# Norm statistics as token columns, spread to rows by TensorE, and two panels multiplied together behind each norm

## The chip, the cores and the metric

The kernel runs on one core of a Trainium2 chip. The metric is the device time of one execution in microseconds, the median of several runs. Lower is better.

## The reference, cut to what matters

The reference is one inference step of a two-layer decoder: 512 prompt tokens and 8 sample tokens, 1024 channels. Only the norms and the products behind them matter here:

```python
def rmsnorm(x, g):
    xf = x.astype(F32)
    y = xf * lax.rsqrt(jnp.mean(xf * xf, axis=-1, keepdims=True) + EPS)
    return y.astype(x.dtype) * g
...
for l in range(DEPTH):                      # two layers
    ...
    o = jnp.concatenate([seq_out, mem_out], axis=-1) @ p['w_out'][l]
    x = x + rmsnorm(o, p['norm_mix_post'][l])
    f, cp = conv_ffn(rmsnorm(x, p['norm_ffn_pre'][l]), p['w_up'][l], ...)
    x = x + rmsnorm(f, p['norm_ffn_post'][l])
```

So a product (w_out or w_down) is normed over the channels and added to x (the post norm), and the new x is normed again (the pre norm) ahead of the next product (w_up, or w_in of the second layer). That happens at four places; behind the last one there is no further product, only the output.

## The kernel before, in words

**Layout.** Activations lie with 128 channels on the partitions: x, y, x_hi and x_lo are tiles of 128 x 8 x 520, eight blocks k of channels by 520 token columns (512 prompt, 8 sample). The columns are worked on in two halves, HALF = (0, 264) and (264, 520).

**Products.** A panel is 128 output channels. A float32 product is made of three products of rounded parts: w_hi with x_hi, w_hi with x_lo, w_lo with x_hi. ScalarE rounds the weights to w_hi (`hi`, L2144), VectorE or GpSimd makes the rest w_lo (`lo`, L1208 on VectorE, L949 on GpSimd), each for a whole panel and in two buffers. Panel q may be rounded when panel q-2 is multiplied (`panel_done`), and multiplied when its w_lo is there and VectorE has read panel q-2 out of its two PSUM banks (`panel_read`).

**A norm.** The mean of squares over the channels is a product with `meanw`, 128 x 128 of 1/1024, as the stationary operand and the squares as the moving one. So the sums stand on every partition, 264 or 256 columns wide. ScalarE takes the root of that tile (`root_half`, L2177), VectorE its reciprocal (`reciprocal_half`, L1219, into rstd), and then VectorE goes through 16 steps (8 blocks of the first half, 8 of the second; `post_norm`): y times gain times rstd (L1738), x + y (L1744), x_lo (L1251), each for one block and half. ScalarE makes x_hi (L2189) and the squares of the new x (L2480) from the same x.

**The order around a norm.** Every engine has its order written out. `last_pair` multiplies the last two panels ahead of a norm half by half, so that the statistics of the first half (`post_stats`, L2700 to L2702) go in while the second half is still multiplied. `first_pair` multiplies the two panels behind it: panel 0 half 0, panel 1 half 0, panel 0 half 1, panel 1 half 1. Panel 0 waits block by block for x_lo (`x_split`), and the sums of the new squares (L2770) go in between. The small numbers (LAST_READ, ROOT_1, HI_NEXT, ROOT_PRE, RECIP_PRE, LO_FIRST, LO_NEXT) say at which of the 16 steps ScalarE or VectorE does a given other piece. Panel 1's weights are rounded at ScalarE's step 8, and its w_lo is made at VectorE's step 11. w_lo of the third panel is made by GpSimd.

**Behind it.** The pre norm's rstd is not applied to x but to the product as VectorE reads it out of PSUM (L1826 and L1827 for w_up). VectorE can start on the first panel only when both halves of that rstd are there.

**PSUM.** Statistics and transposes use a ring of four banks (`misc_jobs` lists the jobs in order, job j uses bank j modulo 4). TensorE takes a bank when the job four places ahead is freed: `take` waits for it. The statistics' bank is freed by ScalarE's root. The last ten jobs are transposes of x for the output (TURNED_OUT: blocks c = 0, 1 with channel halves a = 0, then a = 1; then c = 2, 3, 4 with a = 0, then a = 1); they stand right behind the two statistics jobs of the last norm. ScalarE copies each (L2603) and SyncE stores it.

## Time and profile before

| | us |
|---|---|
| median of 3 runs | 1521.39 (1520.93 to 1525.54) |
| the profiled execution: span, first to last instruction | 1519.0 |
| what lies around the span, against the median | 2.4 |
| TensorE busy with matmuls | 1413.4 (93%) |
| VectorE busy | 976.7 (64%) |
| ScalarE busy | 576.7 (38%) |
| GpSimd busy | 638.5 (42%) |

The profiled execution has no time of its own beside its span, so the span is what the sum is made against, and the median is set beside it. Matmuls are pipelined, so that TensorE's busy time also covers stretches in which it runs at half its clock. Times in the rows below are microseconds from the start of the span.

### The profile page before, as it was taken

The numbers are of one execution on the slowest core, as the hardware profiler recorded it, in microseconds if no ns is written. First come the engines' busy times: TensorE is split into PE (matmuls) and PEld (weight loads), VectorE is DVE, ScalarE is ACT, GpSimd is POOL, SyncE is SP. The second block draws the span as 40 slices with busy tenths as digits, with TensorE's granted clock in tenths as the row PEclk, the third lists the DMA queues.
The fourth block names the chain that finished last, engine by engine and source line by source line (L and its number), as shares of the span: only waits on it lengthen the run. The fifth ranks groups of instructions, "written<-read, shape, count | busy, mean of one in ns | idle before, by whom it ended". The sixth has DMA issues, their size and how long they took to land.

```text
span 1519.0 us, 32537 instructions
## 1 busy us (share of the span) xinstructions
PE 1413.4 (93%) x12097; PEld 1313.9 (86%) x12097; DVE 976.7 (64%) x1658; ACT 576.7 (38%) x1019; POOL 638.5 (42%) x420
## 2 busy tenths in 40 slices
PE   6986978989999999999799989999989999999997
PEld 6984758979999999999699966657889999999997
DVE  5769967576773167765748688753677761376755
ACT  4544354344432133422415235432454431234323
POOL 1586422304444334433177888402223443344430
PEclk9998789989999999999999999999999999999999
DMA  5344364213333232332145769995213233233321
GB/s 173 114 117 79 63 169 123 83 44 85 99 94 98 77 97 83 102 98 75 45 121 164 226 175 308 331 340 157 69 57 97 84 103 90 83 91 88 104 83 62
DMA packets 289082, 180.47 MB, mean 119 GB/s; under 512 B 54248, under 2 KB 274572, under 8 KB 288924
## 3 DMA queue, kind: packets, MB, share of 16 engines
q1 hardware_dynamic: 288412, 179.07, 40.9%
q8 instruction: 61, 1.00, 0.3%
q14 instruction: 33, 0.27, 0.1%
q10 hardware_dynamic: 576, 0.13, 0.0%
HBM read 167.10 MB, written 10.63 MB: 117 GB/s over the span
## 4 chain that ended last, share of the span: by engine, by line
PE 70%; DVE 14%; issue 8%; ACT 2%; SPq 2%; DMA 1%; POOL 1%; DVEq 0%; ACTq 0%; POOLq 0%
PE big L2649 58%; PE big L2715 3%; PE misc L2800 2%; DVE tmp L1261 2%; PE big L2746 2%; DVE y L1738 1%; DVE rstd L1219 1%; DVE x L1744 1%; DVE w_lo L1208 1%; DVE x_lo L1251 1%; SPq L597 1%; PE misc L2770 1%; ACT yc L2506 1%; DVE cp L1261 1%; ACT w_hi L2144 1%
## 5 line engine op out<-in xcount | busy, mean ns | idle before, releaser
L949 POOL TENSOR_TENSOR w_lo<-raw,w_hi 128x1024 fp32r<-128x1024 f32 (+2 forms) x153 | 393.8, 2574 | 708.9 <-ACT w_hi L2144 548.4
L2144 ACT ACTIVATE w_hi<-raw 128x1024 fp32r<-128x1024 f32 (+2 forms) x179 | 198.5, 1109 | 582.1 <-PE big L2649 539.0
L2649 PE MATMUL big<-x_hi,w_hi 128*128 128x264 f32 x1984 | 406.7, 287 | 8.4 <-DVE uc L1827 2.8
L2649 PE MATMUL big<-x_hi,w_lo 128*128 128x264 f32 x1984 | 400.8, 283 | 0.0
L2649 PE MATMUL big<-x_lo,w_hi 128*128 128x264 f32 x1984 | 398.8, 283 | 0.0
L2649 PEld LDWEIGHTS big<-x_hi,w_hi 128*128 128x128 f32 x1984 | 305.9, 189 | 13.1 <-issue 4.7
L2649 PEld LDWEIGHTS big<-x_lo,w_hi 128*128 128x128 f32 x1984 | 305.6, 189 | 0.0
L2649 PEld LDWEIGHTS big<-x_hi,w_lo 128*128 128x128 f32 x1984 | 305.3, 189 | 0.0
L1831 DVE SCALAR_TENSOR_TENSOR yc<-uc,convw,yc 128x512 f32<-128x512 f32 x88 | 136.7, 1554 | 113.2 <-ACT yc L2506 113.2
L2649 PE MATMUL big<-h_hi,w_hi 128*128 128x264 f32 x616 | 125.1, 284 | 6.3 <-DVE h_lo L1846 6.3
L2649 PE MATMUL big<-h_hi,w_lo 128*128 128x264 f32 x616 | 123.9, 282 | 0.0
L2649 PE MATMUL big<-h_lo,w_hi 128*128 128x264 f32 x616 | 123.9, 282 | 0.0
L2649 PEld LDWEIGHTS big<-h_hi,w_hi 128*128 128x128 f32 x616 | 94.1, 188 | 7.4 <-DVE h_lo L1846 7.1
L2649 PEld LDWEIGHTS big<-h_lo,w_hi 128*128 128x128 f32 x616 | 94.4, 188 | 0.0
L2649 PEld LDWEIGHTS big<-h_hi,w_lo 128*128 128x128 f32 x616 | 94.4, 188 | 0.0
L1859 DVE COPY y<-big 128x264 f32 (+1 forms) x32 | 12.2, 424 | 102.6 <-PE big L2649 102.6
L1093 POOL TENSOR_TENSOR areas<-areas,qb 128x768 f32<-128x768 f32 x41 | 74.6, 1830 | 7.0 <-DMA areas<-in_cache_k 6.2
L1836 DVE SCALAR_TENSOR_TENSOR yc<-uc,convw,yc 128x512 f32<-128x512 f32 x88 | 66.2, 752 | 12.7 <-DVE yc L1834 0.2
L2506 ACT ACTIVATE yc<-uc,convw 128x520 f32<-128x520 f32 x88 | 72.3, 821 | 1.1
L1201 DVE TENSOR_TENSOR sumsq<-sumsq,sq 128x520 f32<-128x520 f32 x20 | 52.5, 2627 | 11.7 <-ACT sq L2461 9.9
L2746 PE MATMUL big<-x_hi,w_hi 128*128 128x264 f32 (+1 forms) x96 | 38.4, 400 | 17.8 <-DVE x_lo L1251 10.4
L1219 DVE RECIPROCAL rstd<-sd 128x264 f32<-128x264 f32 (+1 forms) x16 | 28.3, 1773 | 31.5 <-ACT sd L2177 31.5
(434 smaller groups left out, 2330.8 us busy)
## 6 DMA issues: line engine op xcount, KB each, us to landing
raw<-in_w_up SPq DMA_DIRECT2D x88, 512.0 KB, 3.9
raw<-in_w_down SPq DMA_DIRECT2D x32, 704.0 KB, 4.7
areas<-in_cache_k SPq DMA_DIRECT2D x41, 384.0 KB, 4.5
areas<-in_cache_v SPq DMA_DIRECT2D x41, 384.0 KB, 4.7
raw<-in_w_in SPq DMA_DIRECT2D x16, 512.0 KB, 4.2
raw<-in_w_out SPq DMA_DIRECT2D x16, 512.0 KB, 4.2
raw<-in_w_kv SPq DMA_DIRECT2D x12, 512.0 KB, 4.6
spare<-in_cache_k SPq DMA_DIRECT2D x12, 384.0 KB, 4.5
```

The costliest lines, as they stand in the source:

```text
L949: pool.tensor_tensor(w_lo[slot][:, 0:kb, :], raw[slot][:, 0:kb, :], w_hi[slot][:, 0:kb, :].bitcast(F32), ALU.subtract).then_inc(lo_made, 1)
L1093: own.tell(pool.tensor_tensor(p, p, qb[b % 2][:].rearrange("p (a d) -> p a d", a=2), ALU.mult), s_("k_product"), n + 1)
L1201: ins = V.tensor_tensor(sumsq[:], sumsq[:], sq[:, m % 2, :], ALU.add)
L1219: tell(V.reciprocal(rstd[:, c0:c1], sd[:, c0:c1]), s_("rstd_ready"), nstd[0])
L1261: do(V.tensor_tensor(o, a_, b_, op))
L1831: st(V.scalar_tensor_tensor(yy[:, 0:T], uu[:, 1:1 + T], w_[1], yy[:, 0:T], ALU.mult, ALU.add))
L1836: st(V.scalar_tensor_tensor(yy[:, 0:T], uu[:, 0:T], w_[0], yy[:, 0:T], ALU.mult, ALU.add))
L2144: A.activation(w_hi[slot][:, 0:kb, :], raw[slot][:, 0:kb, :], ACT.Copy).then_inc(hi_made, 1)
L2506: A.activation(yy[:], uu[:, 2:2 + NT], ACT.Identity, bias=convw[:, 1 - l, bass.ds(it + (f * KH + half * KF + 132), 1)], scale=convw[:, 1 - ...
L2649: ins = pe.matmul(big[2 * slot + b_][:, 0:c1 - c0], w[slot][:, k, :], r[:, c0:c1], start=(k == 0 and n_ == 0), stop=(k == kb - 1 and n_ == 2))
L2715: return pe.matmul(big[2 * slot + b_][:, 0:c1 - c0], w[slot][:, k, :], r[:, c0:c1], start=(k == 0 and n_ == 0), stop=(k == kb - 1 and n_ = ...
L2746: ins = pe.matmul(big[2 * slot + b_][:, 0:c1 - c0], w[slot][:, k, :], r[:, k, c0:c1], start=(k == 0 and n_ == 0), stop=(k == KD - 1 and n_ ...
```

## The change

Each of the four norms is changed in the same way.

- The statistics' product has its operands the other way round: 128 token columns of the squares are stationary, one column of `meanw` is moving. The result is one column of PSUM with 128 tokens on the partitions, for each block of 128 tokens: three blocks for the first half (the third overlaps and covers the last 8 columns), two for the second. ScalarE takes the root of these 3 or 2 columns (`root_cols`), VectorE the reciprocal (`reciprocal_cols`).
- TensorE spreads them to rows again (`spread_row`): the column, broadcast to 128 x 128, is stationary, the identity is moving. The post norm's row is read by VectorE directly out of PSUM (`stat_row`), and its bank is freed by VectorE when the half's last block is scaled. The pre norm's row is copied to rstd by ScalarE (`copy_row`).
- `first_pair` multiplies the two panels together, block by block: four blocks of panel 0, four of panel 1, then each further block for both.
- Panel 1's weights are rounded at ScalarE's step 2 (was 8), its w_lo is made at VectorE's step 5 (was 11), and w_lo of the third panel is made by VectorE at the end of the norm (was GpSimd, beside it).
- Some semaphores of the start are merged into one (`params_ready`); these hunks are left out.

```diff
@@ -148,6 +148,20 @@
+def stat_blocks(n):
+    c0, c1 = HALF[n]
+    full_ = [(c0 + P * j, P * j, 0) for j in range((c1 - c0) // P)]
+    over = (c1 - c0) % P
+    return full_ + ([(c1 - P, c1 - c0 - over, P - over)] if over else [])
+ROW = 8
@@ -195,8 +209,9 @@
-ROOT_1, HI_NEXT, ROOT_PRE, RECIP_PRE = 6, 8, 10, 13
-LO_FIRST, LO_NEXT = 1, 11
+RECIP_1, ROOT_1, HI_NEXT, ROOT_PRE, RECIP_PRE, ROWS_PRE = 6, 4, 2, 9, 11, 12
+LO_FIRST, LO_NEXT, LAST_READ_END = 1, 5, 5
+LAG = 4
@@ -582,6 +597,16 @@
+        def stat_cols_at(i, n):
+            c = 8 * (i % 4)
+            w = len(stat_blocks(n))
+            return sd[:, c:c + w], sd[:, 32 + c:32 + c + w]
+        def stat_row(job):
+            return bank(job)[:, ROW:ROW + HALF[job[2]][1] - HALF[job[2]][0]]
@@ -1125,11 +1150,13 @@
                 done = 22 * int(name[2]) + 11 * int(name[3])
-                for i in range(2 if name[3] == "0" else 0, 4):
+                for i in range(3 if name[3] == "0" else 0, 4):
                     if i == 3:
...
                         pool.wait_ge(s_("h_made"), done + 1)
+                    if i == 3 and name[3] == "0":
+                        pool.wait_ge(lo_made, base + 3)
                     lo(base + i, (base + i) % 2, kb)
@@ -1139,7 +1166,8 @@
                 if name == "win1":
-                    for i in range(2, n):
+                    pool.wait_ge(lo_made, base + 3)
+                    for i in range(3, n):
                         lo(base + i, (base + i) % 2, kb)
@@ -1218,6 +1246,25 @@
+            ncol = [0]
+            def reciprocal_cols(n):
+                root, recip = stat_cols_at(ncol[0], n)
+                ncol[0] += 1
+                dve.wait_ge(s_("root_cols"), ncol[0])
+                tell(V.reciprocal(recip, root), s_("rstd_ready"), 3 + ncol[0])
+            def row_spread(i):
+                dve.wait_ge(s_("row_spread"), i)
+            def rows_read(name):
+                for n in range(2):
+                    _, _, read, before = place(("ms", name, n))
+                    dve.wait_ge(read, before + 1)
@@ -1723,24 +1770,31 @@
                 sync()
-                reciprocal_half(stats, 0)
-                sync()
-                read_half(ph, 6, 1, add)
+                last_read = LAST_READ if nxt is not None else LAST_READ_END
+                reciprocal_cols(0)
+                first = ncol[0]
+                row_spread(first)
                 steps = [k for _, k in by_half()]
...
                 for i in range(2 * KD + 2):
+                    if i == (RECIP_1 if nxt is not None else KD):
+                        reciprocal_cols(1)
                     if i == KD:
-                        reciprocal_half(stats, 1)
-                        sync()
+                        row_spread(first + 1)
                     if i < 2 * KD:
...
                         c = slice(*HALF[n])
-                        tell(V.scalar_tensor_tensor(y[:, k, c], y[:, k, c], gain(name, k, l), rstd[:, c], ALU.mult,
-                                                    ALU.mult), s_("y_scaled"), done + i + 1)
+                        tell(V.scalar_tensor_tensor(y[:, k, c], y[:, k, c], gain(name, k, l),
+                                                    stat_row(("ms", stats, n)), ALU.mult, ALU.mult),
+                             s_("y_scaled"), done + i + 1)
+                    if i == 0:
+                        read_half(ph, 6, 1, add)
                     if 1 <= i <= 2 * KD:
...
                         dve.wait_ge(s_("y_scaled"), done + i)
+                        if k == KD - 1:
+                            dve.sem_inc(place(("ms", stats, n))[2], 1)
                         tell(V.tensor_tensor(x[:, k, c], x[:, k, c], y[:, k, c], ALU.add), s_("x_updated"), done + i)
@@ -1750,14 +1804,15 @@
                         lo(PH[ph][2] + 9)
-                    if i == LAST_READ:
+                    if i == last_read:
                         read_half(ph, 7, 1, add)
...
                     if nxt is not None and i == RECIP_PRE:
-                        reciprocal_half(stat_name[1], 0)
+                        reciprocal_cols(0)
                 if nxt is not None:
-                    reciprocal_half(stat_name[1], 1)
-                    sync()
+                    reciprocal_cols(1)
+                    lo(PH[ph][2] + 10)
+                    rows_read(stat_name[1])
@@ -2176,6 +2231,21 @@
+            ncol = [0]
+            def root_cols(name, n):
+                job, (root, _) = ("ms", name, n), stat_cols_at(ncol[0], n)
+                ncol[0] += 1
+                full(act, job)
+                tell(A.activation(root, bank(job)[:, 0:len(stat_blocks(n))], ACT.Sqrt, bias=eps[:, 0:1]),
+                     s_("root_cols"), ncol[0])
+            def copy_row(name, n, i):
+                act.wait_ge(s_("row_spread"), i)
+                freed(own, A.activation(rstd[:, slice(*HALF[n])], stat_row(("ms", name, n)), ACT.Copy), ("ms", name, n))
@@ -2465,7 +2535,7 @@
                 square_half(ph, 7, 0)
-                root_half(name, 0)
+                root_cols(name, 0)
                 if (ph, name) != ("down11", "d1"):
@@ -2480,14 +2550,17 @@
                         square_half(ph, 7, 1)
-                    elif i == ROOT_1:
-                        root_half(stats, 1)
-                    elif i == HI_NEXT:
+                    if i == ROOT_1:
+                        root_cols(stats, 1)
+                    if i == HI_NEXT:
                         hi(PH[after][0], base + n + 1)
-                    elif i == ROOT_PRE:
-                        root_half(name, 0)
+                    if i == ROOT_PRE:
+                        root_cols(name, 0)
+                    if i == ROWS_PRE:
+                        copy_row(name, 0, ncol[0])
+                root_cols(name, 1)
                 hi(KD, base + n + 2)
-                root_half(name, 1)
+                copy_row(name, 1, ncol[0])
                 ny[0] += 1
@@ -2695,11 +2768,27 @@
                     pe.wait_ge(s_("sq_used"), 2 + 6 * npost[0])
-                o, (c0, c1) = take(("ms", name, n)), HALF[n]
+                o = take(("ms", name, n))
                 pe.wait_ge(s_("sq_last"), 4 * npost[0] - 2 + 2 * n)
-                pe.matmul(o[:, 0:c1 - c0], meanw[:], sumsq[:, c0:c1], start=True, stop=False)
-                pe.matmul(o[:, 0:c1 - c0], meanw[:], sq[:, 0, c0:c1], start=False, stop=False)
-                give(pe.matmul(o[:, 0:c1 - c0], meanw[:], sq[:, 1, c0:c1], start=False, stop=True), ("ms", name, n))
+                for j, (at, _, _) in enumerate(stat_blocks(n)):
+                    t = slice(at, at + P)
+                    pe.matmul(o[:, j:j + 1], sumsq[:, t], meanw[:, 0:1], start=True, stop=False)
+                    pe.matmul(o[:, j:j + 1], sq[:, 0, t], meanw[:, 0:1], start=False, stop=False)
+                    ins = pe.matmul(o[:, j:j + 1], sq[:, 1, t], meanw[:, 0:1], start=False, stop=True)
+                give(ins, ("ms", name, n))
+            nrow = [0]
+            def spread_row(name, n):
+                i, o = nrow[0], bank(("ms", name, n))
+                nrow[0] += 1
+                pe.wait_ge(s_("rstd_ready"), 3 + i + 1)
+                _, recip = stat_cols_at(i, n)
+                for j, (_, at, skip) in enumerate(stat_blocks(n)):
+                    ins = pe.matmul(o[:, ROW + at:ROW + at + P - skip], recip[:, j:j + 1].to_broadcast([P, P]),
+                                    ident[:, skip:P], start=True, stop=True)
+                ins.then_inc(s_("row_spread"), 1)
@@ -2723,6 +2812,8 @@
                                 post_stats(stats, 0)
+                        if b_ == 1 and p_ == 0:
+                            spread_row(stats, 0)
                         if b_ == 0:
@@ -2732,29 +2823,54 @@
...
+                def ready(p_):
+                    pe.wait_ge(lo_made, base + p_ + 1)
+                    pe.wait_ge(panel_read, base + p_ - 1)
+                def block(p_, b_, k):
+                    slot, (c0, c1) = (base + p_) % 2, HALF[b_]
+                    for n_, (w, r) in enumerate(((w_hi, x_hi), (w_hi, x_lo), (w_lo, x_hi))):
+                        ins = pe.matmul(big[2 * slot + b_][:, 0:c1 - c0], w[slot][:, k, :], r[:, k, c0:c1],
+                                        start=(k == 0 and n_ == 0), stop=(k == KD - 1 and n_ == 2))
+                    if b_ and k == KD - 1:
+                        ins.then_inc(panel_done, 1)
+                ready(0)
+                for k in range(LAG):
+                    x_split(k)
+                    block(0, 0, k)
+                    if k == LAST_READ:
+                        post_stats(before, 1)
+                    if k >= LAST_READ:
+                        add(0, k - LAST_READ)
+                ready(1)
+                for k in range(LAG):
+                    block(1, 0, k)
+                add(0, LAG - LAST_READ)
+                spread_row(before, 1)
+                for k in range(LAG, KD):
+                    x_split(k)
+                    block(0, 0, k)
+                    block(1, 0, k)
+                    add(0, k - 1)
+                add(0, KD - 1)
+                for k in range(KD):
+                    if k == KD - 1:
+                        add(1, k - 1)
+                        add(1, k)
+                    x_split(KD + k)
+                    block(0, 1, k)
+                    if k >= LAG:
+                        block(1, 1, k - LAG)
+                    if 1 <= k < KD - 1:
+                        add(1, k - 1)
+                    if k == LAG - 1:
+                        spread_row(name, 0)
+                block(1, 1, LAG)
+                spread_row(name, 1)
+                for k in range(LAG + 1, KD):
+                    block(1, 1, k)
@@ -2763,11 +2879,12 @@
                 def add(n, k):
-                    c0, c1 = HALF[n]
                     if k == 0:
...
                     pe.wait_ge(s_("xsq_made"), done + KD * n + k + 1)
-                    ins = pe.matmul(o[n][:, 0:c1 - c0], meanw[:], y[:, k, c0:c1], start=(k == 0), stop=(k == KD - 1))
+                    for j, (at, _, _) in enumerate(stat_blocks(n)):
+                        ins = pe.matmul(o[n][:, j:j + 1], y[:, k, at:at + P], meanw[:, 0:1], start=(k == j == 0),
+                                        stop=(k == KD - 1 and at + P == HALF[n][1]))
                     if k == KD - 1:
@@ -3377,6 +3494,7 @@
             post_stats("d1", 1)
+            spread_row("d1", 1)
             for c, a_ in TURNED_OUT:
...
                 o = take(("yT", c, a_))
```

## Rows read from the trace of the kernel before

**Rows 1.** The page's chain of work that ended last, shares by engine.
```profile
PE 70%; DVE 14%; issue 8%; ACT 2%; SPq 2%; DMA 1%; POOL 1%; DVEq 0%; ACTq 0%; POOLq 0%
```
**Rows 2.** Timeline, TensorE, first norm: start, duration, engine, line, operation, count, [idle, releaser].
```profile
305.99 0.68 PE L2700 MATMUL misc<-sumsq,meanw 128*128 128x264 f32 x2
...
307.20 0.47 PE L2715 MATMUL big<-x_hi,w_hi 128*128 128x256 f32 x1
...
310.96 1.11 PE L2715 MATMUL big<-x_hi,w_lo 128*128 128x256 f32 x8
314.09 0.37 PE L2746 MATMUL big<-x_hi,w_hi 128*128 128x264 f32 x1 [2.02 <-DVE x_lo L1251]
...
321.89 0.61 PE L2770 MATMUL misc<-y,meanw 128*128 128x264 f32 x2
...
322.71 0.61 PE L2770 MATMUL misc<-y,meanw 128*128 128x264 f32 x2
...
328.67 0.59 PE L2746 MATMUL big<-x_hi,w_hi 128*128 128x264 f32 x1 [2.36 <-DVE w_lo L1208]
...
345.63 0.51 PE L2649 MATMUL big<-x_hi,w_hi 128*128 128x264 f32 x2 [1.42 <-DVE uc L1827]
```
**Rows 3.** Timeline, VectorE, the same norm.
```profile
310.42 0.89 DVE L1738 SCALAR_TENSOR_TENSOR y<-y,gains,rstd 128x264 f32<-128x264 f32 x2
...
311.57 1.22 DVE L1208 TENSOR_TENSOR w_lo<-raw,w_hi 128x1024 fp32r<-128x1024 f32 x1
...
316.21 0.49 DVE L1251 SCALAR_TENSOR_TENSOR x_lo<-x,gains,x_hi 128x264 fp32r<-128x264 f32 x1
...
317.37 0.49 DVE L1251 SCALAR_TENSOR_TENSOR x_lo<-x,gains,x_hi 128x264 fp32r<-128x264 f32 x1
...
321.01 1.75 DVE L1219 RECIPROCAL rstd<-sd 128x256 f32<-128x256 f32 x1 [0.85 <-ACT sd L2177]
322.80 0.49 DVE L1738 SCALAR_TENSOR_TENSOR y<-y,gains,rstd 128x256 f32<-128x256 f32 x1
...
342.68 1.75 DVE L1219 RECIPROCAL rstd<-sd 128x256 f32<-128x256 f32 x1 [4.68 <-ACT sd L2177]
```
**Rows 4.** Timeline, ScalarE, the same norm: the weights of panel 0 are rounded.
```profile
309.31 1.06 ACT L2144 ACTIVATE w_hi<-raw 128x1024 fp32r<-128x1024 f32 x1 [1.17 <-PE big L2715]
```
**Rows 5.** Timeline, TensorE: first and third panel's start, second and third norm.
```profile
725.32 0.36 PE L2746 MATMUL big<-x_hi,w_hi 128*128 128x264 f32 x1 [0.21 <-DVE x_lo L1251]
...
756.68 0.48 PE L2649 MATMUL big<-x_hi,w_hi 128*128 128x264 f32 x2 [2.38 <-DVE qs L1946]
...
1093.07 0.36 PE L2746 MATMUL big<-x_hi,w_hi 128*128 128x264 f32 x1 [2.02 <-DVE x_lo L1251]
...
1121.85 0.51 PE L2649 MATMUL big<-x_hi,w_hi 128*128 128x264 f32 x2 [1.41 <-DVE uc L1827]
```
**Rows 6.** Timeline, TensorE: three float32 products with two moving columns.
```profile
1041.77 0.80 PE L3314 MATMUL misc<-rowsel,rstd 128*128 128x2 f32 x6
```
**Rows 7.** Groups by line and form, TensorE (those products) and VectorE (a small reciprocal).
```profile
L3314 PE MATMUL misc<-rowsel,rstd 128*128 128x2 f32 x48 | 6.6, 254 | 2.7 <-DVE x_lo L1509 1.9 <-DVE rstd L2050 0.7
...
L1497 DVE RECIPROCAL ast<-ast 128x8 f32<-128x8 f32 x10 | 2.0, 201 | 2.2 <-PE misc L3032 1.9 <-DVE hp L1635 0.2
```
**Rows 8.** Stretches of the first norm: length, busy by engine, granted clock, DMA.
```profile
312.00:328.70 16.70, 11.42 (x46) 8.63 (x45) 15.78 (x35) 10.16 (x25) 0.00 (x0) 0.77 0.11 32
328.70:335.00 6.30, 6.30 (x27) 6.09 (x28) 4.53 (x10) 1.89 (x5) 0.00 (x0) 0.52 0.34 87
```
**Rows 9.** Timeline of the end, VectorE: last panel read, second half's first step.
```profile
1501.34 0.42 DVE L1770 TENSOR_TENSOR y<-y,big 128x256 f32<-128x256 f32 x1 [1.52 <-PE big L2715]
...
1507.32 0.48 DVE L1738 SCALAR_TENSOR_TENSOR y<-y,gains,rstd 128x256 f32<-128x256 f32 x1
```
**Rows 10.** Timeline of the end, TensorE: the last six transposing jobs.
```profile
1511.13 5.09 PE L2800 MATMUL misc<-ident,x 128*128 128x128 f32 x24 [1.64 <-DVE x L1744]
```
**Rows 11.** Timeline of the end, ScalarE: the last two copies.
```profile
1515.69 1.30 ACT L2603 ACTIVATE ytok<-misc 128x512 f32<-128x512 f32 x2 [0.26 <-PE misc L2800]
```

More of the change, by code:

```diff
@@ L2734, in first_pair @@
                 add = x_stats(name)
-                for b_, (c0, c1) in enumerate(HALF):
-                    for p_ in range(2):
-                        q = base + p_
-                        slot = q % 2
-                        if b_ == 0:
-                            pe.wait_ge(lo_made, q + 1)
-                            pe.wait_ge(panel_read, q - 1)
-                        for k in range(KD):
-                            if p_ == 0:
-                                x_split(KD * b_ + k)
-                            for n_, (w, r) in enumerate(((w_hi, x_hi), (w_hi, x_lo), (w_lo, x_hi))):
-                                ins = pe.matmul(big[2 * slot + b_][:, 0:c1 - c0], w[slot][:, k, :], r[:, k, c0:c1],
-                                                start=(k == 0 and n_ == 0), stop=(k == KD - 1 and n_ == 2))
-                            if b_ == 0 and p_ == 0 and k == LAST_READ:
-                                post_stats(before, 1)
-                                add(0, 0)
-                                add(0, 1)
-                            elif p_ == 0 and k > (0 if b_ else LAST_READ):
-                                add(b_, k - 1)
-                            elif p_ == 1 and k == 1:
-                                add(b_, KD - 1)
-                        if b_:
-                            ins.then_inc(panel_done, 1)
```

15 lines of the change are left out of this document (8 added, 7 removed).

## The prediction, made before the changed kernel ran

> **What bounds the kernel now.** I read the page's chain of waits first. TensorE holds 70% of it, VectorE 14% [rows 1]. VectorE's part comes largely from the four norms, so I then read the timelines of TensorE, VectorE and ScalarE around each norm, and the stretches with their clock. The reader is to see four things.
>
> First, TensorE waits twice behind a norm: 2.02 us for the first x_lo and 2.36 us for panel 1's w_lo [rows 2]. A third wait, 1.42 us, ends when VectorE has read the first new panel, because the pre norm's last reciprocal (342.68, 1.75 us) is late [rows 2, 3].
>
> Second, a wide reciprocal takes 1.75 us, and each norm has two for the post norm and two for the pre norm [rows 3].
>
> Third, TensorE's clock falls behind these waits. It was granted 0.77 of full speed from 312.0 to 328.7 and 0.52, the lower of the two levels (1.2 GHz), from 328.7 to 335.0 [rows 8].
>
> Fourth, the distance from the first block of panel 0 to the first product of the third panel is what a norm costs the chain: 345.63 - 314.09 = 31.5 us, 756.68 - 725.32 = 31.4 us and 1121.85 - 1093.07 = 28.8 us for the first three norms [rows 2, 5]. Behind the third panel the kernel goes on in the same rhythm wherever it starts, so what is won there is kept. The fourth norm runs straight into the output.
>
> **The price of a column product.** A float32 product is issued as two pieces (x2 in each row). Today one x statistics product takes two pieces of 264 columns; from one such pair to the next it is 322.71 - 321.89 = 0.82 us, with three panel matmuls between [rows 2]. Eight of those started 1.11 - 0.28 = 0.83 us apart in all, 0.12 each (the first to the eighth; 0.28 is the length of one in the neighbouring rows) [rows 2], so the product itself costs 0.82 - 0.36 = 0.46. In the new form 128 x 128 squares are loaded for each moving column. The nearest rows have two moving columns behind such a load: six pieces in 0.80 us, one alone 0.254, so (0.80 - 0.25) / 5 = 0.11 us apart [rows 6, 7]. I take 0.11. The upper bound is 0.80 / 6 = 0.13, in case each group pays its start and end. The lower bound is 0.055, in case a single column halves it; nothing in a row speaks for it. So a sum over the first half costs 3 blocks x 2 pieces x 0.11 = 0.65, over the second 0.43: what was 0.46 becomes 0.54 on average, and the post statistics go from 6 pieces to 18 or 12.
>
> The Trainium skill (TensorE: Matmul & The Clock Gate, Back-to-back issue gap) gives about 81 ns for a sustained pair of weight load and matmul with 128 moving columns, set by both. The float32 pieces here were 0.11 apart with only two columns, so the trace does not agree; by the skill's figure some 106 pieces behind a norm would be 3 us cheaper, 9 us over three norms, an estimate.
>
> **Last pair ahead of a norm.** The statistics of half 0 took 307.20 - 305.99 = 1.2 us plus about 0.2 in the next matmul [rows 2]; 18 pieces take 1.9. The row spread adds 6 pieces of 128 columns, 0.65. TensorE is thus 1.2 us later at the end of the pair. For that, VectorE's first scaling comes earlier. Root (0.2) and small reciprocal (at most 0.20 [rows 7]) run beside the six matmuls left, the spread ends near 309.5, and the first scaling starts near 309.6 instead of 310.42 [rows 3]. But the next thing in VectorE's order is w_lo of panel 0. It needs w_hi, and ScalarE rounds that when panel 0 of the last pair is done: 309.31 [rows 4], now 1.2 later, finished near 311.5. w_lo started at 311.57 [rows 3], and starts there again. The 0.8 us won is lost to this wait, and TensorE's 2.02 us of idleness only shrinks because its work is longer. First x_lo: 0 in norms 1 and 3. In norm 2 TensorE had only 0.21 us of slack [rows 5], so it starts 1.0 us later.
>
> **First pair, at full clock, from the first block.** + stands for time after that block's start. VectorE gives one x_lo each 1.16 us (317.37 - 316.21 [rows 3]), with one longer step. Blocks 0 to 2 are done at +3.0. Then follow post statistics 12 x 0.11 = 1.3 (+4.3), sum 0.65, block 3 0.36, sum 0.65 (+6.0), four blocks of panel 1 1.45, sum 0.65, spread 0.45 (+8.5). VectorE's scaling of half 1 starts at about +8.7, as before (322.80 - 314.09 = 8.7 [rows 2, 3]): the removed reciprocal (321.01) pays for w_lo of panel 1, which now lies ahead. Four double blocks with a sum each, 4 x (0.72 + 0.65), and one more sum: +14.7. VectorE meanwhile stops at step 11 for the small reciprocal, so that x_lo of the third block of half 1 is there at +16.4. Blocks 0 and 1 (+15.8), a wait, blocks 2 and 3 (+18.4), spread 0.65, blocks 4 to 6 at 0.72 + 0.43 each (+22.5), two sums and block 7 (+23.8): panel 0 is done. The new tail is a chain: hop 0.1, w_hi 1.06 [rows 4], w_lo 1.22 on VectorE [rows 3] (GpSimd had made it beside), and the reading of the first panel, 345.63 - 344.43 = 1.2 (342.68 + 1.75 is the end of the reciprocal [rows 2, 3]): +27.4. The remaining matmuls (2.3 us) lie beside it. Waits for w_lo of panel 1 (2.36 us) are gone; TensorE is the bound instead.
>
> So at full clock the distance is 27.4 in norms 1 and 3. In norm 2 it is 28.5: 0.3 for a later second block, 0.8 because VectorE reads a whole w_in panel there. Against today that is -4.1, then -2.9 + 1.0 (later start) = -1.9, and -1.4: together -7.4.
>
> **The clock.** The waits between the first three blocks remain (0.8 ahead of the first, then 1.15 and 0.8). After such a series the clock was low in norms 1 and 3. TensorE is now the bound behind them, so a low stretch costs up to half its length. In 312.0 to 328.7 the mean of 0.77 is 7.7 us at half speed, (1 - 0.77) / 0.5 x 16.7; the whole of 328.7 to 335.0 was low [rows 8]. The second has no cause any more. Of the first I take half, 3.8 us, of which the waits hide some: +1.3 in norms 1 and 3, and +0.8 in norm 2, whose early waits were the shortest. Together +3.4. The bounds are 0 and, for the whole 7.7, 2.7 a norm.
>
> **The end.** The fourth norm's bank is no longer freed by ScalarE's root, but by VectorE at its last scaling of that half. The ring has four banks, and the fourth transposing job (c = 1, a = 1) uses the bank of the statistics of half 1. So it and the six behind it wait for VectorE's step 16. The last panel was read at 1501.34 and scaling of half 1 began at 1507.32 [rows 9]. Now the read is at about 1502.6 (last pair +1.2); then come the read and its square 0.9, 12 pieces 1.3, root and reciprocal 0.4, spread 0.45 and hops 0.8: 1506.4. The bank is free when all eight blocks are scaled, 8 x 0.75 later (two operations of about 0.4 without x_lo), 1512.4. Then seven jobs instead of six are left: six took 5.09 us for 24 pieces at 0.21 [rows 10], 0.85 a job. 1512.4 + 7 x 0.85 = 1518.4, and the last copy starts there instead of near 1516.4 [rows 11]: +2.0. At full clock ScalarE's 0.65 a copy (1.30 for two [rows 11]) sets the pace, and it is +0.5. TensorE will have stood still for over 4 us, longer than ahead of the slow row shown, so low is likely: I take +1.8.
>
> **Sum.** -7.4 + 3.4 + 1.8 = -2.2 on a span of 1519.0: 1516.8. The median lies 2.4 above the span, so 1519.2. The merged start semaphores and small operands cost nothing: none is in the way of TensorE.
>
> **Rivals.**
> (a) The clock stays full behind all norms. For it: TensorE works without a long wait from block 3 on, and the 2.36 us wait goes. Against it: the early waits are nearly those of today. -7.4 + 0.5 to 1.8: 1514.5 to 1515.8.
> (b) The other side, slower: the clock falls, or does not rise again, while column pieces are mixed with panel products. TensorE's 24 us behind a norm then lengthen by half of the part that is low beyond full speed: with two thirds of it low, 16 us more, of which 8 lie in TensorE's waits, so +8 a norm: -7.4 + 24 + 2.0 = +19, 1540. It decides once more than some 8 us of a norm are low. Against it: the two-column pieces in the attention kept 0.11 [rows 6].
> (c) Low clock for the whole 7.7 us in each norm, and pieces at 0.13: -7.4 + 8.1 + 2.0 + 3 x 106 x 0.02 = +9, of which I take half as more likely than all: about 1526.
> (d) The bank wait at the end does not matter, because the transposes catch up: -4.0, 1517.4. Against it: seven jobs stand behind one semaphore.
> (e) Column pieces are a quarter cheaper, because the load of the next runs beside the one ahead: 106 x 0.03 x 3 = 9.5 less, 1510. By the Trainium skill's figure, named above (TensorE: Matmul & The Clock Gate), it would be so. Against it are the rows at 0.11.
>
> **Chances.** The forecast, with (d), 0.56; (a) 0.20; (e) 0.04; (c) 0.12; (b) 0.08. A measurement of this kernel can tell a change of about 0.3%, 4.6 us, from none: the bounds are 1516.8 and 1526.0. Faster is (a), (e) and the lower edge of the forecast, 0.31; slower is (b) and half of (c), 0.14; same 0.55. The range leaves out (e), (b) and the far ends of (a) and (c): 1513.5 to 1525.5.
>
> **What would show it.** Right: reciprocals on the chain gone; TensorE from first block to third panel 27 to 30 us in all three norms with no wait above 1.5 us in between; w_lo of panel 0 starting when w_hi ends; at the end a TensorE wait of over 4 us ending with VectorE's last scaling, then seven jobs. Wrong: column pieces not 0.11 apart at full clock; granted clock low for more than 7 us per norm, or nowhere; VectorE rather than TensorE waited for in half 0; the last transposes starting before VectorE's last step.

## The result, and the profile after

| | before | changed |
|---|---|---|
| median us of 4 executions each (lowest to highest) | 1523.47 (1520.93 to 1530.24) | 1569.88 (1567.27 to 1571.33) |
| ratio, 95% interval | | 1.0293 [1.0272, 1.0315] |
| profiled execution: time, span | span 1519.0 | 1567.27, span 1565.3 |

The change made the kernel 2.9% slower. The prediction was 1519.2 with a range of 1513.5 to 1525.5. It was wrong.

The chain of waits after, by engine, answers to [rows 1]. TensorE's share has risen from 70% to 77% and VectorE's has fallen.

```profile
PE 77%; DVE 12%; issue 4%; ACT 2%; SPq 2%; DMA 2%; POOL 2%; DVEq 0%; ACTq 0%; POOLq 0%
```

TensorE's timeline in the first norm (start, duration, line, operation, count, [idle before it, releaser]) answers to [rows 2]:

```profile
303.49 0.35 PE L2775 MATMUL misc<-meanw,sumsq 128*128 128x1 f32 x2
303.71 0.36 PE L2776 MATMUL misc<-meanw,sq 128*128 128x1 f32 x2
...
305.49 0.36 PE L2804 MATMUL big<-x_hi,w_hi 128*128 128x256 f32 x1
...
311.86 0.36 PE L2834 MATMUL big<-x_hi,w_hi 128*128 128x264 f32 x1 [0.87 <-DVE x_lo L1298]
...
313.37 0.39 PE L2834 MATMUL big<-x_hi,w_hi 128*128 128x264 f32 x1 [0.91 <-DVE x_lo L1298]
...
314.52 0.39 PE L2834 MATMUL big<-x_hi,w_hi 128*128 128x264 f32 x1 [0.52 <-DVE x_lo L1298]
...
314.99 0.28 PE L2775 MATMUL misc<-meanw,sumsq 128*128 128x1 f32 x2
315.13 0.56 PE L2776 MATMUL misc<-meanw,sq 128*128 128x1 f32 x2
...
326.72 1.27 PE L2886 MATMUL misc<-meanw,y 128*128 128x1 f32 x6
327.85 0.57 PE L2834 MATMUL big<-x_hi,w_hi 128*128 128x264 f32 x1
...
356.26 0.51 PE L2722 MATMUL big<-x_hi,w_hi 128*128 128x264 f32 x2
```

The first block starts at 311.86, the third panel at 356.26: a distance of 44.4 us where it was 31.5. No wait stands between 315 and 356. But at 315.13 a pair of one-column pieces takes 0.56 instead of the 0.36 it took at 303.71, ahead of the norm. Six of them from 326.72 to the next product are 0.19 apart. Ahead of the norm 18 pieces took 305.49 - 303.49 = 2.0 us, 0.11 each.

The stretches of the same norm, then of norms 2 and 3 (from:to, length, busy time of TensorE, its weight loads, VectorE, ScalarE, GpSimd, granted clock, DMA share, GB/s), answer to [rows 8]:

```profile
301.50:310.00 8.50, 8.50 (x74) 8.41 (x72) 2.92 (x7) 2.53 (x7) 0.00 (x0) 1.00 0.26 65
315.00:325.00 10.00, 10.00 (x50) 10.00 (x49) 4.28 (x10) 3.39 (x10) 0.00 (x0) 0.51 0.22 57
325.00:343.00 18.00, 18.00 (x85) 18.00 (x85) 8.85 (x24) 5.05 (x13) 0.00 (x0) 0.50 0.00 0
343.00:356.00 13.00, 13.00 (x63) 13.00 (x62) 3.75 (x10) 4.20 (x10) 0.00 (x0) 0.50 0.01 1
356.30:366.00 9.70, 9.70 (x82) 9.70 (x82) 6.91 (x15) 5.61 (x8) 2.57 (x2) 1.00 0.39 106
...
745.00:776.00 31.00, 31.00 (x146) 31.00 (x145) 10.72 (x29) 7.91 (x22) 0.00 (x0) 0.50 0.01 4
...
1130.00:1160.00 30.00, 30.00 (x141) 30.00 (x141) 10.55 (x28) 7.87 (x21) 0.00 (x0) 0.50 0.00 1
```

The reader is to see two columns together: TensorE is busy all the time, and its granted clock is 0.50, the lower of the two levels (1.2 GHz). It is at 1.00 ahead of the norm and again once only panel products run. In stretches of a quarter of a microsecond it is low from 315.0 to 356.2, from 741.8 to 779.5 and from 1124.0 to 1165.2: 41, 38 and 41 us. The first and third panels of norms 2 and 3 answer to [rows 5]:

```profile
736.60 0.32 PE L2834 MATMUL big<-x_hi,w_hi 128*128 128x264 f32 x1
...
781.02 0.47 PE L2722 MATMUL big<-x_hi,w_hi 128*128 128x264 f32 x2 [1.08 <-DVE qs L2001]
...
1121.21 0.36 PE L2834 MATMUL big<-x_hi,w_hi 128*128 128x264 f32 x1 [0.87 <-DVE x_lo L1298]
...
1165.93 0.51 PE L2722 MATMUL big<-x_hi,w_hi 128*128 128x264 f32 x2 [0.20 <-DVE uc L1882]
```

The three distances grew by 12.9, 13.1 and 15.9, together 41.9 of the 46.3 us by which the span grew. The rest: the first norm began 2.2 earlier, norm 2 0.65 later behind norm 1, the attention between norms 2 and 3 took 3.8 more (of that below), and the end, from norm 3's third panel on, took 399.4 instead of 397.2.

VectorE now waits for TensorE, for the spread row (misc) or through ScalarE's root (sd) of sums that TensorE had made late (the same norm; the row's bracket is the idle time):

```profile
307.14 0.49 DVE L1787 SCALAR_TENSOR_TENSOR y<-y,gains,misc 128x264 f32<-128x264 f32 x1 [0.93 <-PE misc L2789]
...
309.34 1.22 DVE L1236 TENSOR_TENSOR w_lo<-raw,w_hi 128x1024 fp32r<-128x1024 f32 x1
...
325.64 0.48 DVE L1787 SCALAR_TENSOR_TENSOR y<-y,gains,misc 128x256 f32<-128x256 f32 x1 [5.46 <-PE misc L2789]
...
337.40 0.18 DVE L1256 RECIPROCAL sd<-sd 128x3 f32<-128x3 f32 x1 [7.16 <-ACT sd L2241]
```

The reciprocals are indeed small, 0.18 us instead of 1.75 [rows 3]. What they saved is not on the path any more: VectorE stands still for 5.46 and 7.16 us.

### The profile page after: what moved, and what is told of

It is laid out like the page before. It is cut to its first block, busy times and chain, and to the rows that moved or that the text cites. A ratio compares the mean times of both kernels' runs of the same rounds, so it can differ in the third digit from the quotient of the medians.

```text
span 1565.3 us, 33106 instructions
## 1 busy us (share of the span) xinstructions
PE 1474.8 (94%) x12383; PEld 1382.8 (88%) x12383; DVE 957.0 (61%) x1661; ACT 575.8 (37%) x1025; POOL 631.9 (40%) x417
## 4 chain that ended last, share of the span: by engine, by line
PE 77%; DVE 12%; issue 4%; ACT 2%; SPq 2%; DMA 2%; POOL 2%; DVEq 0%; ACTq 0%; POOLq 0%
PE big L2722 54%; PE big L2834 4%; PE big L2804 3%; PE misc L2886 3%; PE misc L2917 2%; DVE tmp L1308 2%; SPq L622 1%; PE big L3115 1%; PE misc L3416 1%; PE misc L3149 1%; DVE cp L1308 1%; PE big L2917 1%; PE misc L2789 1%; POOL w_lo L974 1%; PE misc L3332 1%
## 5 line engine op out<-in xcount | busy, mean ns | idle before, releaser
L974 POOL TENSOR_TENSOR w_lo<-raw,w_hi 128x1024 fp32r<-128x1024 f32 (+2 forms) x150 | 386.9, 2579 | 762.4 <-ACT w_hi L2199 492.3
L2886 PEld LDWEIGHTS misc<-meanw,y 128*128 128x128 f32 x240 | 55.5, 330 | 0.0
L2834 PE MATMUL big<-x_hi,w_hi 128*128 128x264 f32 (+1 forms) x96 | 45.6, 475 | 6.5 <-DVE x_lo L1298 6.5
```

What stands on the lines that cost most here:

```text
L974: pool.tensor_tensor(w_lo[slot][:, 0:kb, :], raw[slot][:, 0:kb, :], w_hi[slot][:, 0:kb, :].bitcast(F32), ALU.subtract).then_inc(lo_made, 1)
L2834: ins = pe.matmul(big[2 * slot + b_][:, 0:c1 - c0], w[slot][:, k, :], r[:, k, c0:c1], start=(k == 0 and n_ == 0), stop=(k == KD - 1 and n_ ...
L2886: ins = pe.matmul(o[n][:, j:j + 1], y[:, k, at:at + P], meanw[:, 0:1], start=(k == j == 0), stop=(k == KD - 1 and at + P == HALF[n][1]))
```

## The experiments

**Theory 1:** the one-column pieces between panel products bring TensorE's clock down and keep it there. **Theory 2:** the new order with its early waits does. **Theory 3:** it is the number of pieces and weight loads. "Distance" is always from a norm's first block to the third panel, from one profiled execution, norms 1, 2, 3. Before: 31.5, 31.4, 28.8. Changed: 44.4, 44.4, 44.7. The medians of the kernel before beside the experiments were 1524 to 1526; each ratio compares with them. Code is cut to what matters: `...` stands for what is left out, and the comments are added here.

**Wide pieces in the same places.**

```diff
-pe.matmul(o[:, j:j + 1], sumsq[:, t], meanw[:, 0:1], start=True, stop=False)
+c = slice(STAT + WIDE * j, STAT + WIDE * j + WIDE)      # WIDE = 80
+pe.matmul(o[:, c], sumsq[:, t], meanw[:, 0:WIDE], start=True, stop=False)
...                                     # and so for sq and for the x sums
```

> The changed kernel with one edit: each statistics piece multiplies 80 columns of meanw instead of one (the same number of pieces and of weight loads; ScalarE's root takes one column of each 80). Theory 1 (the one-column pieces keep TensorE's clock at its lower level although it is never idle): the granted clock behind norms is near full, first block to third panel is 27 to 30 us instead of 44.4, 44.4 and 44.7, and the time is 1514 to 1524. Theory 2 (the new order with its early waits lowers the clock) and theory 3 (it is the number of pieces, or of weight loads, whatever their clock): the distances stay at 43 to 46 and the time at 1565 to 1572.

Measured: 1533.9 us, ratio 1.006 [1.0039, 1.0082]; distances 31.5, 32.8, 33.0. The number of instructions is the same (12383 matmuls), only their columns differ, and 36 us are gone. Theories 2 and 3 fall as the main cause. But a low stretch is left, right behind the three early waits (this kernel's stretches, columns as above):

```profile
320.20:327.00 6.80, 6.80 (x34) 6.80 (x34) 4.34 (x10) 3.45 (x10) 0.00 (x0) 0.51 0.29 79
...
327.00:348.00 21.00, 19.54 (x162) 18.88 (x161) 12.16 (x33) 9.28 (x23) 0.00 (x0) 0.99 0.01 2
```

From 327 on, 80-column pieces between the same panel products leave the clock at 0.99 where one-column pieces had it at 0.50. The time is 10 us over the upper end of what was expected, and the distances are 1.5 to 3 us over theirs. `v2_busy_tail` (below), without these low stretches, has 10.9 us less in the three distances.

**The old order with column pieces.** The changed kernel, `first_pair` with the old loops:

```diff
-for k in range(LAG, KD):
-    x_split(k); block(0, 0, k); block(1, 0, k); add(0, k - 1)
...
+for b_ in range(2):
+    for p_ in range(2):
+        for k in range(KD):
+            block(p_, b_, k)         # sums and spreads in between
```

> The changed kernel with column statistics and row spreads, but the two panels behind a norm in the old order, one half of a panel after the other. Theory 1 (one-column pieces): the clock is low as in the changed kernel, wherever column pieces lie between panel products; the distance is 40 to 48 us and the time 1555 to 1585. Theory 2 (the new order): the distance is back at 30 to 33 us and the time at 1520 to 1530. Theory 3 (number of pieces): as theory 1 in the distance, but with the granted clock no lower than in the kernel before.

Measured (2 runs): 1562.0 us; distances 42.0, 43.1, 41.3; from 318 to 342 the granted clock was 0.53. As theory 1 has it: the old order alone does not bring the time back. In norm 1 the clock came back to 1.00 at 340.8, behind a row of panel products with no column piece between them (337.1 to 340.6), and fell again at 347.4 among the column pieces.

**The new order alone.** The kernel before, wide statistics, new `first_pair`, HI_NEXT = 2, LO_NEXT = 5.

> The kernel before with only the new order: panel 0 and panel 1 behind a norm together block by block, panel 1's weights rounded at ScalarE's step 2 and their w_lo at VectorE's step 5. Statistics, roots and reciprocals stay wide; the third panel's w_lo stays with GpSimd. Theory 1: the clock behaves as before or better, the 2.36 us wait for panel 1's w_lo is gone, the late pre reciprocal (1.75 us) stays: distances 28 to 31 us, time 1514 to 1522. Theory 2 (the order lowers the clock): distances 40 us and more, time 1545 to 1570.

Measured: 1526.65 us, ratio 1.0017 [1.0005, 1.003]; distances 29.3, 30.3, 29.3. The order does what it should for the distance, 2.9 us in all against the first profile of before, and the clock is low only from about 316 to 322, as in before. VectorE's wide reciprocals bound it now: TensorE waits 1.69 us for x_lo and 2.7 to 3.7 us ahead of the third panel. The time missed what was expected (1514 to 1522) and is, if anything, longer than before; two profiles of before (below) say how little 3 us in one profile mean here.

**One-column pieces added to the kernel before.** The additional products are work that nobody reads.

```diff
 ins = pe.matmul(o[n][:, 0:c1 - c0], meanw[:], y[:, k, c0:c1], ...)
+for j in range(3 - n):
+    at = c0 + P * j if j < 2 else c1 - P
+    ins = pe.matmul(o[n][:, 300 + j:301 + j], y[:, k, at:at + P], meanw[:, 0:1], ...)
```

> The kernel before with additional work: behind each wide x statistics product three (first half) or two (second half) one-column products whose results nobody reads, 80 pieces a norm as in the changed kernel. Everything else, the order included, is that of before. Theory 1: the clock falls while these pieces are mixed in, 80 pieces cost 8.8 us at full clock and the 20 us around them are up to twice as long: the distance goes from 31.5, 31.4 and 28.8 us to 48 to 56, the time to 1565 to 1595. Theory 3 (only their number counts): +8.8 us a norm at most, 1540 to 1548. Theory 2 (the new order is to blame): as theory 3, since the order is unchanged.

Measured (2 runs): 1529.97 and 1549.68 us; distances 34.4, 34.9, 33.9. The distances and the rows are those of the first run, the profiled one. In it theory 1 as I had put it missed: the clock was low for the first microseconds, as in before, and then 1.00 with the pieces in (TensorE of this kernel):

```profile
321.40 0.72 PE L2773 MATMUL misc<-meanw,y 128*128 128x1 f32 x6
321.98 0.37 PE L2746 MATMUL big<-x_hi,w_hi 128*128 128x264 f32 x1
...
322.43 0.61 PE L2770 MATMUL misc<-y,meanw 128*128 128x264 f32 x2
322.87 0.72 PE L2773 MATMUL misc<-meanw,y 128*128 128x1 f32 x6
```

Between two groups of six column pieces (six in 0.58 us) stand three panel products and a wide pair. In the changed kernel, at full clock, there would be the panel products alone. So in this run the mere presence of the pieces was not enough. That they do the harm because they stand in place of the wide products is an inference; whether it is their share of the time or the wide pair's columns this kernel can't tell. The second run speaks against a firm rule: it was 19.7 us longer (the kernel before spread over 12 us in 19 executions), and its mean granted clock was 0.961 where the first had 0.976. By these means it spent (0.039 x 1547.8 - 0.024 x 1528.0) / 0.5 = 47 us more at the lower level, which costs up to half of that, 24 us, an estimate. Where that was is not known; it may have been behind the norms.

**Column pieces where TensorE had not waited.** Theory A: they suffice. Theory B: a wait has to come first.

```diff
+def fill():
+    for j in range(3):
+        pe.matmul(big[2 * slot + b_][:, 300 + j:301 + j], ident[:], meanw[:, 0:1], ...)
 for k in range(kb):
     part(k, 0)
     part(k, 1)
+    if k % 2 == 1: fill()
...
+            if k == kb // 2: fill()
```

> The kernel before with additional one-column products ahead of each norm, where TensorE had no wait for over 20 us: in the last pair of panels six pieces stand behind every fourth or fifth panel product (120 pieces for each of the four norms, results unused); in the changed kernel six pieces stand behind every third or sixth. Theory A (one-column pieces among panel products alone are enough to bring the clock down): the granted clock falls to 0.5 in the last pair, which takes 38 to 50 us instead of 12. Theory B (the clock falls only behind TensorE's waits, and the column pieces then keep it from rising): the granted clock stays at 1.0 up to the first wait, the last pair takes 25 us (12 + 120 x 0.11), and the time is 1570 to 1580, all of it work at full clock.

Measured (one run): 1619.7 us. The additional pieces are 120 ahead of norms 1 and 3 and 144 ahead of norms 2 and 4, where the product has 11 blocks instead of 8 (528 in all). The first norm's last pair took from 300.13 to 342.98, 42.9 us. TensorE of this kernel, ahead of the norm:

```profile
300.61 0.73 PE L2723 MATMUL big<-meanw,ident 128*128 128x1 f32 x6
301.20 0.37 PE L2715 MATMUL big<-x_hi,w_hi 128*128 128x264 f32 x1
...
302.94 0.73 PE L2723 MATMUL big<-meanw,ident 128*128 128x1 f32 x6
...
304.04 0.42 PE L2715 MATMUL big<-x_lo,w_hi 128*128 128x264 f32 x1
304.26 1.28 PE L2723 MATMUL big<-meanw,ident 128*128 128x1 f32 x6
```

No row has a bracket: TensorE had not been idle, and it was busy for all of 270 to 300 as well. The panel product goes from 0.28 to 0.42 us and six pieces from 0.73 to 1.28 at 304. The mean granted clock from 304 to 330 was 0.54. Ahead of norm 3 it was the same (0.50 from 1133 to 1172). Ahead of norms 2 and 4, with six pieces behind every fourth panel product there too, it was not:

```profile
740.00:764.00 24.00, 24.00 (x204) 23.80 (x204) 6.03 (x10) 3.52 (x7) 0.03 (x1) 1.00 0.15 44
...
1566.00:1599.00 33.00, 32.99 (x280) 32.59 (x279) 8.93 (x12) 4.48 (x8) 3.18 (x1) 1.00 0.03 7
```

Norm 2's last pair ran at full clock for 29 us and fell to 0.50 for its last 8, norm 4's did not fall at all. So theory B is out, since the clock fell three times with no wait ahead. Theory A holds only in part: this mixture can bring the clock down by itself, at once, or after 29 us, or not at all in 33 us, and what decides between these is open. The Trainium skill (TensorE: Matmul & The Clock Gate, HAM oscillation — how this bites in real kernels) puts a kernel's falls of the clock down to TensorE's waits for DMA; this trace does not agree with waits as the only cause.

**Only the post norm in columns.** The pre norm (80 of the 110 pieces) is wide again, roots and reciprocals too; then the same with the 30 left at 80 columns.

```diff
-for j, (at, _, _) in enumerate(stat_blocks(n)):
-    ins = pe.matmul(o[n][:, j:j + 1], y[:, k, at:at + P], meanw[:, 0:1], ...)
+ins = pe.matmul(o[n][:, 0:c1 - c0], meanw[:], y[:, k, c0:c1], ...)
...
-reciprocal_cols(1)
+reciprocal_pre(stat_name[1], 1)      # wide, in place in rstd
```

> The changed kernel with the pre norm's statistics as in the kernel before: wide x sums (two pieces of 264 columns), wide root and wide reciprocal, no row copies. Only the post norm keeps columns and row spreads, 30 one-column pieces a norm instead of 110. The new order stays. Theory 1 (it is the 80 one-column pieces between the panel products that keep the clock down): the clock is low only for the first 8 to 12 us behind a norm, as in the kernel before, the distances are 29 to 33 us and the time 1518 to 1528. If the post norm's pieces alone are enough, or the waits of the new order: distances 38 us and more, time over 1550.

> As the kernel with the pre norm wide, but the post norm's pieces multiply 80 columns of meanw instead of one. If the post norm's twelve one-column pieces behind the early waits bring the clock down for longer, this one is 1 to 3 us a norm faster than that one; if the low stretch comes from the early waits alone, the two agree within 1 us a norm. Distances 28 to 31 us, time 1515 to 1525.

Measured: 1542.9 us, ratio 1.0118 [1.0082, 1.0154], distances 32.2, 33.6, 32.2; with 80 columns 1538.9, ratio 1.0092 [1.0057, 1.0126], distances 32.2, 33.5, 32.1. The two agree within 0.2 us a norm: the post norm's twelve pieces alone do no lasting harm. The distances are up to 0.6 and 2.5 us over what was expected, the times 14 to 15 us over the upper ends. Of the 24 and 22 us that the spans are over before, the profiles place 6 in the distances, 9 and 6 in the attention (345.7 and 342.5 us against 336.4), 4 at the end (401.7 and 401.0) and the rest ahead of norms 1 and 2. The changed kernel's end is 2.2 us longer too, and the same wait for the bank stands in both (3.26 and 4.24 us ahead of the last seven jobs). The rest fits a low stretch right behind norm 3's third panel (granted clock 0.72 from 1141.3 to 1147.5, and 0.71 from 1139.7 to 1145.5), which before did not have; why it is there is open.

**The bank at the end.** The changed kernel, last norm only:

```diff
+copy_row("d1", 1, ncol[0])          # ScalarE: rstd <- the row in PSUM, frees the bank
...
-stat_row(("ms", stats, n))
+stat_row(("ms", stats, n)) if nxt is not None or n == 0 else rstd[:, c]
```

> The changed kernel with one edit in the last norm: the row of the second half is copied out of PSUM by ScalarE, as the pre norms' rows are, and VectorE reads the copy. So the bank is free some 6 us earlier. If the bank is what holds the last transposes (the predicted step), TensorE's wait of 3.5 us ahead of seven jobs goes, and from the third panel of norm 3 to the end it is 397 to 398.5 us instead of 399.4, the time about 1568. If the transposes wait for something else, the stretch stays at 399.4 or grows by the copy (0.5 us).

Measured (one run): 1569.0 us; from the third panel to the end 396.0 us instead of 399.4, better than expected. TensorE at the end of the changed kernel, then of this one:

```profile
1549.91 0.71 PE L2789 MATMUL misc<-ident,sd 128*128 128x128 f32 x4 [0.55 <-DVE sd L1256]
1550.46 2.45 PE L2917 MATMUL misc<-ident,x 128*128 128x128 f32 x12
1556.44 5.47 PE L2917 MATMUL misc<-ident,x 128*128 128x128 f32 x28 [3.52 <-DVEq L1797]
```

```profile
1555.34 3.48 PE L2922 MATMUL misc<-ident,x 128*128 128x128 f32 x16
1559.77 1.53 PE L2922 MATMUL misc<-ident,x 128*128 128x128 f32 x12 [0.95 <-DVE x L1802]
1562.30 1.53 PE L2922 MATMUL misc<-ident,x 128*128 128x128 f32 x12 [1.00 <-DVE x L1802]
```

Three jobs (12 pieces), a wait of 3.52 us for VectorE's last scaling, seven jobs (28 pieces): the predicted picture. With the copy this wait is gone and the jobs follow VectorE block by block. The clock has a part in the gain: it was 0.51 from 1550.5 to 1561 in the changed kernel, and here 1.00 from 1559.5 to 1564.

**Products in the early waits.** The low 7 us that are left in the kernel with 80 columns begin behind three waits. Additional products, results unused, fill them; `v2_busy_tail` has the 80 columns and the bank's copy as well.

```diff
+def busy(m, alone=False):
+    for _ in range(m):
+        pe.matmul(big[2 * slot][:, 264:512], w_hi[slot][:, 0, :],
+                  w_hi[slot][:, 0:2, :]...[:, 0:248], start=alone, stop=alone)
 ready(0)
+busy(7, True)                        # none in norm 2
 for k in range(LAG):
+    if k in (1, 2): busy(8 if k == 1 else 5)        # 11 in norm 2
     x_split(k)
```

> The changed kernel with three edits together: statistics pieces with 80 columns, the last norm's second row copied by ScalarE, and additional products of rounded weights (248 columns, results unused, 0.12 us each) while TensorE would otherwise wait for the first three x_lo behind a norm: 7 ahead of the first block (none in norm 2), 8 (11 in norm 2) ahead of the second, 5 ahead of the third. Theory W (TensorE's waits there bring the clock down): the low 7 us behind each norm that the kernel with 80 columns still has go, the distances fall from 31.5, 32.8 and 33.0 us to 27.5 to 30, the end is 396.0 instead of 399.3, the time 1519 to 1524. Rival (the statistics pieces, even with 80 columns, bring the clock down by themselves): the low stretch stays, distances 31 to 33.5, time 1528 to 1532.

> The changed kernel, its one-column pieces untouched, with the same additional products in the three early waits. If one-column pieces among the panel products are enough by themselves (as ahead of a norm in the kernel before), the clock still falls within a few microseconds of the post statistics and stays low: distances 40 to 45 us, time 1555 to 1570. If the early waits are needed for the fall, it stays high: distances 27 to 31, time 1520 to 1530.

> The kernel before with the new order alone, and with the additional products in the early waits (15 ahead of the first block, none in norm 2; then 8 or 11, and 5). Theory W: the 7 us of low clock behind each norm go. TensorE is not the bound in this form (VectorE's wide reciprocals are: TensorE waits 1.7 us for x_lo later and 2.7 to 3.7 us ahead of the third panel), so the distance falls only from 29.3, 30.3 and 29.3 us to 27.5 to 28.5, and the time is 1520 to 1525. Rival: the low stretch stays and so do the distances.

Measured: `v2_busy_tail` 1523.1 us (10 runs) against 1526.2, ratio 0.9964 [0.9945, 0.9984]; distances 28.4, 29.7, 28.4. Its stretches, norm 1 and norm 2:

```profile
315.00:343.00 28.00, 26.20 (x215) 25.22 (x215) 19.79 (x52) 15.06 (x38) 0.00 (x0) 1.00 0.15 40
...
724.00:753.00 29.00, 26.28 (x218) 25.28 (x216) 20.95 (x52) 15.79 (x38) 0.54 (x1) 1.00 0.13 36
```

The clock is 1.00 throughout, in norm 3 too (1096 to 1124). So the low stretch of the kernel with 80 columns hangs on TensorE's waits: filled, they leave it out. With both causes gone, the distances are 5.2 us below the first profile of before. This version beats the kernel before by 0.4% and the changed one by some 3%.

`e9_busy_1col` (one run): 1559.0 us; distances 41.5, 35.0, 41.8. The clock still falls, only later, and in norm 1 with no idle time of TensorE from 312 to 358:

```profile
312.00:324.00 12.00, 11.94 (x99) 11.44 (x98) 10.34 (x24) 7.05 (x16) 0.00 (x0) 1.00 0.16 44
...
325.00:350.00 25.00, 25.00 (x119) 25.00 (x118) 10.69 (x29) 8.14 (x22) 0.00 (x0) 0.50 0.07 15
```

In the changed kernel it fell 3.1, 5.2 and 2.8 us behind the first block, here 6.6, 18.1 and 6.3 us behind it. So in these executions the waits brought the fall forward, but the pieces were enough for it and kept the clock low. Norm 2's 35.0 is below what I expected; there the clock was 1.00 up to 757.5.

`v4_order_busy`: 1525.7 us, ratio 1.0007 [0.9986, 1.0027]; distances 28.7, 30.3, 28.7; granted clock 1.00 from 314 to 330. Time and distances are slightly over what was expected. Against the new order alone (1526.65 us, distances 29.3, 30.3, 29.3) the clock came back and the time did not move: VectorE is the bound of that form. A full clock is worth something only where TensorE is waited for.

**The kernel before once more.**

> The kernel before, unchanged, profiled a second time. The stretch from norm 2's third panel to norm 3's first block (attention) took 336.4 us in its first profile and 340 to 346 us in the changed kernel and five of the experiments, where the granted clock was at 0.5 for three or four short stretches more. If that is chance of the single execution, this profile may show 336 to 343 us and other low stretches than the first one; if it belongs to the other kernels' timing, it shows 336 to 337 us with the same low stretches, and all three distances at 31.5, 31.4 and 28.8 either way.

Measured (one run): 1527.0 us; distances 30.2, 31.2, 30.3 (sum 91.6, first profile 91.7); attention 340.5 us. The single distances expected to stand did not; their sum did. The short low stretches in the attention (beginning 266, 276 and 290 us behind the third panel, in the first profile only one, at 264) come and go with the execution. So the 3.8 of the 46.3 us need not be an effect of the change. The two spans are 1519.0 and 1525.0: the span of a single profile can't tell changes of less than some 6 us. Single stretches agree better: the end took 397.2 and 396.8 us, so that the 2.2 and 3.4 us found there are clear of this.

## Why the prediction was wrong

- **The step that failed is "The clock".** It took the low stretch of before, 7.7 us, halved it and got +3.4 us in all. The low stretches were 41, 38 and 41 us long (315 to 356 in norm 1) and lasted while column pieces stood among the panel products and a few microseconds more. With 80 columns in a piece and the waits filled, at full clock, the distances are 28.4, 29.7, 28.4 (`v2_busy_tail`), so the low clock cost 16.0, 14.7 and 16.3 us: 47, where +3.4 stood.
- Why it failed: I read the clock as a matter of TensorE's waits alone, because the low stretches that the prediction looked at stood behind waits. The narrow pieces behind a norm were priced by time (0.11 each) and not by what they do to the clock.
- **Rival (b) named the mechanism** with a chance of 0.08. Its size was short: +8 a norm, for it let a third of the stretch be at full clock and took the waits off; by the same comparison it was 15 to 16. The row held against it, six two-column pieces at 0.11 [rows 6], was a single short group: it shows their price at full clock and says nothing on 40 us of pieces among panel products.
- **Full-clock distance** (27.4, 28.5, 27.4): right within 1.2 us each, as far as `v2_busy_tail` can show it: it has 28.4, 29.7, 28.4, but with products in the waits, 80 columns and no one-column pieces.
- **Price of a piece, 0.11 at full clock**: right (18 in 2.0 us). Rival (e) falls.
- **Last pair**: right. VectorE's first scaling starts 10.7 us behind the pair's first product (307.14 - 296.42; 11.5 before, 10.7 predicted), and w_lo of panel 0 starts at 309.34, when ScalarE's w_hi ends; norm 2 begins 0.65 us later (predicted 1.0), in norms 1 and 3 the last pair takes 15.4 instead of 15.2 us up to the first block.
- **The end** (+1.8): right in picture and nearly in size (+2.2); the wait for the bank was 3.52 us, where over 4 was given as a sign. Undone, it gives 3.4.
- **What would show it wrong** had the sign that came: a granted clock low for more than 7 us per norm. The others did not come: the pieces were 0.11 apart at full clock, the last transposes waited for VectorE's last step, and behind the first three blocks TensorE was the bound, as predicted, with VectorE idle for 5.46 and 7.16 us.
- Rivals (a), (c) and (d): the clock was neither full nor low for only 7.7 us a norm, and the bank wait did matter.

## What to carry to other kernels

Turning a product round so that its result is one column wide trades VectorE time for TensorE pieces with one moving column. In this kernel many of them among other products cost the clock of everything around them; look at the granted clock of the stretch, not at the busy share, which stayed at 100%. If such a form is wanted, give the pieces more columns than they need (a piece took 0.11 us at full clock with 1 and with 80) and keep useful or useless products in TensorE's short waits (`v2_busy_tail`, with the bank's copy too, 1523.1 us against 1533.9 for the columns alone), but only where TensorE is what the path waits for.

## What was not expected of the hardware

- The granted clock stood at 0.50 for 41 us with TensorE busy all the time. There it fell behind three short waits; ahead of norms 1 to 3 in the kernel with additional pieces in the last pair, and in norm 1 of `e9_busy_1col`, it fell with no wait ahead.
- One column or 80: a piece took 0.11 us at full clock either way, and only with 80 did the clock come back (0.99 from 327 on) with the pieces still there.
- Column pieces did not bring it down in the one profiled run where a wide pair stood in each group beside them, and nearly the same mixture of pieces and panel products brought it down at once, after 29 us, or not at all. Which property of the mixture decides is open.
- 20 unused products behind a norm (16 in norm 2), some 2.4 us of TensorE's waits, took away the 7 us of low clock that the kernel with 80 columns had in norm 1.
